# Three more slabs of a mixer split in parts, and the first transfers and products of the kernel rearranged

## The reference, cut to what matters

```python
x = first_block(...)        # rms_norm, w_in, three attentions, gates, w_out, MLP
# second block
xn = rmsnorm(h, mix_norm_w)
proj = xn @ w_in
xa, qkv, z, beta_logit, a_logit, gate_a, gate_b = split(proj)
y_a = pool_mixer(xa, pool_w, pool_scale) @ w_pool_up      # trailing means over 2, 4, 8, 16 tokens
y_b = deltanet_branch(qkv, z, beta_logit, a_logit, ...) @ w_dn_up   # causal conv, silu, l2norm, delta rule
merged = sigmoid(gate_a) * y_a + sigmoid(gate_b) * y_b
h = h + merged @ w_mix_out
h = h + peer_ffn(rmsnorm(h, ffn_norm_w), ...)             # 128 expert rows a token
return rmsnorm(h, final_norm_w)
```

## Time and profile before

| what | value |
|---|---|
| median of three runs | 1455.67 us |
| the profiled execution | 1455.38 us |
| its span on the core | 1453.6 us |
| TensorE busy | 1302.1 us, 90% of the span |
| VectorE busy | 899.7 us, 62% |
| GpSimd busy | 645.7 us, 44% |
| ScalarE busy | 460.9 us, 32% |
| chain that ended last | 58% TensorE, 28% DMA |

### The profile page before, as it was taken

How to read it: one execution, slowest core, us unless ns; L and a number is a source line. 1 busy time by engine, 2 the same in 40 slices (tenths; PEclk the granted TensorE clock), 3 DMA queues, 4 the chain that set the end, 5 groups by cost and what they waited for, 6 DMA issues and landing times.

```text
span 1453.6 us, 17543 instructions
## 1 busy us (share of the span) xinstructions
PE 1302.1 (90%) x6502; PEld 947.6 (65%) x6502; DVE 899.7 (62%) x1720; ACT 460.9 (32%) x843; POOL 645.7 (44%) x394
## 2 busy tenths in 40 slices
PE   5999998999989999999999997788878898776877
PEld 5997987998879999999975553344334443232332
DVE  3244244999945966432627776676776777667654
ACT  3664524444344534112101322222222222222222
POOL 5553235889936613321203534443444445444430
PEclk9999999999999999999999999999999999999998
DMA  7724343445543433122406999999999999999994
GB/s 264 288 86 168 117 158 132 174 174 199 207 174 117 174 146 117 65 110 88 141 34 266 422 423 420 422 421 422 422 421 421 422 421 421 421 422 421 422 421 170
DMA packets 54203, 389.90 MB, mean 268 GB/s; under 512 B 5208, under 2 KB 13544, under 8 KB 14440
## 3 DMA queue, kind: packets, MB, share of 16 engines
q0 software_dynamic: 36864, 268.45, 44.4%
q1 hardware_dynamic: 14720, 116.40, 21.4%
q10 hardware_dynamic: 2536, 3.95, 0.8%
HBM read 387.70 MB, written 1.07 MB: 267 GB/s over the span
## 4 chain that ended last, share of the span: by engine, by line
PE 58%; DMA 28%; DVE 5%; issue 3%; POOL 2%; ACT 1%; ACTq 0%; DVEq 0%; POOLq 0%
PE psum L506 57%; DMA work<-experts_dram,work 21%; DMA weight_ring<-experts_dram,work 6%; DVE work L1747 2%; POOL work L2329 1%; PE psum L675 1%; ACT work L2161 0%; POOL weight_ring L2329 0%; DMA bias_rows_dram<-work 0%; ACT work L1972 0%; DVE work L1544 0%; PE psum L903 0%; DVE work L1736 0%; DVE work L1734 0%; POOL norm_stats L2234 0%
## 5 line engine op out<-in xcount | busy, mean ns | idle before, releaser
L506 PE MATMUL psum<-work 128*128 128x128 f32 (+6 forms) x1880 | 446.7, 394 | 65.0 <-ACT work L2161 64.7
L506 PEld LDWEIGHTS psum<-work 128*128 128x128 f32 (+2 forms) x1880 | 265.7, 193 | 236.9 <-issue 150.8
L2244 POOL TENSOR_TENSOR weight_lo<-weight_ring,weight_hi 128x2048 fp32r<-128x2048 f32 x62 | 291.9, 4708 | 175.8 <-ACT weight_hi L1827 159.9
L2329 POOL DMA_INDIRECT work<-experts_dram,work x153 | 171.3, 1119 | 216.7 <-PE psum L506 180.4
L1747 DVE CUSTOM_DVE_ANT_0 work<-work 128x1024 f32<-128x1024 f32 x153 | 187.5, 1226 | 109.7 <-DMA work<-experts_dram,work 96.7
L506 PE MATMUL psum<-weight_ring,work 128*128 128x512 f32 (+1 forms) x448 | 200.8, 593 | 42.1 <-ACT work L2161 42.1
L506 PEld LDWEIGHTS psum<-weight_ring,work 128*128 128x128 f32 (+1 forms) x448 | 81.6, 186 | 147.9 <-issue 85.6
L506 PE MATMUL psum<-normed_T,weight_ring 128*128 128x256 f32 (+1 forms) x768 | 156.5, 362 | 1.7 <-ACT normed_T L1827 1.7
L1827 ACT ACTIVATE weight_hi<-weight_ring 128x2048 fp32r<-128x2048 f32 x66 | 125.8, 1915 | 89.6 <-DMA weight_ring<-weights_dram 79.3
L506 PEld LDWEIGHTS psum<-normed_T,weight_ring 128*128 128x128 f32 x768 | 135.6, 190 | 22.8 <-issue 5.3
L506 PE MATMUL psum<-mlp_in_hi,weight_hi 128*128 128x256 f32 x504 | 144.9, 290 | 5.6 <-POOL weight_lo L2244 5.6
(11 more groups left out here) (263 smaller groups left out, 1736.9 us busy)
## 6 DMA issues: line engine op xcount, KB each, us to landing
weight_ring<-weights_dram SPq DMA_DIRECT2D x50, 2048.0 KB, 7.9
work<-weights_dram SPq DMA_DIRECT2D x3, 1024.0 KB, 6.4
work<-experts_dram,work POOLq DMA_INDIRECT x153, 20.3
weight_ring<-weights_dram SPq DMA_DIRECT2D x2, 1024.0 KB, 13.4
gain_rows<-gains_dram SPq DMA_DIRECT2D x2, 1024.0 KB, 10.2
work<-bias_rows_dram ACTq DMA_DIRECT2D x2, 1024.0 KB, 10.5
weight_ring<-experts_dram,work POOLq DMA_INDIRECT x80
constants<-constants_dram ACTq DMA_DIRECT2D x1, 1094.0 KB, 9.5
```

The lines of the kernel that those rows point to most:

```text
L506: return nc.tensor.matmul(o, l, r, start=start, stop=stop)
L2244: G_.tensor_tensor(low, loaded, high.bitcast(F32), ALU.subtract).then_inc(S("weight_lo_ready"), 1)
L2329: G_.indirect_dma_start(out=slots[s], out_offset=None, in_=experts, in_offset=bass.IndirectOffsetOnAxis(ap=expert[:, n % UNIT_BUFS, i:i + ...
```

## The change

In the second mixer:

- xa, gate2_b0 and gate2_b1 are multiplied split too. Six halves (66 to 71) are added, each with a high part by ScalarE and a low part by GpSimd. Their homes are 22528, 26624, 24576, 16480, 0 and 2048 of `work`.
- u2_hi moves to offset 12384 of `work`, u2_lo to the area of the gain rows. The second transfer of the gains moves from slab 40 to slab 44 and waits for gate2_b1.
- The gate logits (`beta_a`) and the first two square sums are computed in parts of 64 tokens.

At the start:

- x is loaded in two transfers, one for each tile. ScalarE squares each tile; there is a root for each; VectorE makes a scaled diagonal of 128 x 128, and TensorE multiplies the residual by it. `normed` and the functions `mean_squares` and `scaled` go.
- VectorE makes both parts of half 0. ScalarE makes u_hi, VectorE u_lo.
- The first projection goes through `first_features`, in the order high·high, low·high, high·low, each group with its own waits.
- The large part of the constants is loaded on SP behind slab 1, not on ScalarE's queue at the start.
- k_att is computed ahead of the bias rows, on TensorE and on ScalarE.

The words that came with the change say that the input's two transfers are joined; the diff has one transfer before and two after, and the diff is what is taken here.

```diff
-    + tuple((31 + s, f"qkv{s}", "features") for s in range(6))
+    + tuple((31 + s, f"qkv{s}", "features") for s in range(6)) \
+    + ((37, "xa", "features"), (38, "gate2_b0", "features"), (39, "gate2_b1", "features"))
+XA_HALF = QKV_HALF + 12
-DVE_HALVES = (5, MLP_HALF + 1, QKV_HALF, QKV_HALF + 1)
+DVE_HALVES = (0, 5, MLP_HALF + 1, QKV_HALF, QKV_HALF + 1)
-    + [(22528, 26624, 24576)[h % 3] for h in range(SPLIT_HALVES - QKV_HALF)]
+    + [(22528, 26624, 24576)[h % 3] for h in range(XA_HALF - QKV_HALF)] + [22528, 26624, 24576, 16480, 0, 2048]
-    u2_hi = split_part("mixer_in_hi", "work", 18528, [P, KC, SEQ])
-    u2_lo = split_part("mixer_in_lo", "work", 16480, [P, KC, SEQ])
+    u2_hi = split_part("mixer_in_hi", "work", 12384, [P, KC, SEQ])
+    u2_lo = split_part("mixer_in_lo", "gain_rows", 0, [P, KC, SEQ])
...
+            def first_features(name, after):
+                for i in range(2):
+                    h = next_half()
+                    _, lo, hi = half_views(h)
+                    ps = open_bank(name, i)
+                    if h == 0:
+                        pe.wait_ge(S("vector_weight_hi_ready"), 1)
+                    else:
+                        pe.wait_ge(S("weight_hi_ready"), h)
+                    for a in range(2):
+                        f, o = slice(a * P, (a + 1) * P), ps[:, a * SEQ:(a + 1) * SEQ]
+                        for k in range(KC):
+                            if i == a == 0 and k % 2 == 0:
+                                pe.wait_ge(S("mix_hi_ready"), k // 2 + 1)
+                            mm(o, hi[:, k, f], u_hi[:, k, :], k == 0, False)
+                        if a == 0:
+                            low_ready(h)
+                        for k in range(KC):
+                            mm(o, lo[:, k, f], u_hi[:, k, :], False, False)
+                        for k in range(KC):
+                            if i == a == 0 and k % 2 == 0:
+                                drained(pe, after, k // 2)
+                            ins = mm(o, hi[:, k, f], u_lo[:, k, :], False, k == KC - 1)
+                    close_bank(ins, name, i)
+                slab_read(name, 1)
...
-            transposes("mix_T", normed, norm=0)
-            split_features("q_nsa", after="mix_T")
+            transposes("mix_T", h_tok, norm=0, scale=mix_scale)
+            first_features("q_nsa", "mix_T")
+            split_features("k_att", groups=3)
...
-                        if s < 2:
-                            ins = mm(ps[:, cols], square_buf[:, s % 2, a, t * P:(t + 1) * P], C("ones")[:, 0:2])
-                        else:
-                            for c in range(2):
...
+                        for c in range(2):
+                            tokens, r = slice(t * P + c * CHUNK, t * P + (c + 1) * CHUNK), (c if s < 2 else 1 - c) * CHUNK
+                            ins = mm(ps[r:r + CHUNK, cols], square_buf[:, s % 2, a, tokens], C("ones")[:, 0:2])
...
-            feature_major("xa", uT, KC)
+            split_features("xa", src=(u2_hi, u2_lo))
...
-            feature_major("gate2_b0", uT, KC)
+            split_features("gate2_b0", src=(u2_hi, u2_lo))
...
-            feature_major("gate2_b1", uT, KC)
+            split_features("gate2_b1", src=(u2_hi, u2_lo))
...
@@ scalar @@
-                    if s < 4 or (s, i) == (4, 0):
-                        weight_high(QKV_HALF + 3 + 2 * s + i)
+                    weight_high(QKV_HALF + 3 + 2 * s + i)
...
             for i in range(2):
                 ps = full(act, "xa", i).rearrange("p (a n) -> p a n", a=2)
                 free(copy(xa[:, 2 * i:2 * i + 2, 16:272], ps), "xa", i)
+                if i == 0:
+                    weight_high(XA_HALF + 3)
             silu(5)
+            weight_high(XA_HALF + 4)
...
             A.activation(k_dec, k_dec, ACT.Exp).then_inc(S("e_factors_ready"), 1)
             landed(act, "e_factors_ready")
+            weight_high(XA_HALF + 5)
...
@@ gpsimd @@
-            for h in range(DVE_HALVES[3] + 1, SPLIT_HALVES):
+            for h in range(DVE_HALVES[4] + 1, XA_HALF):
                 weight_low(h)
             for kind in range(2):
+                for h in ((XA_HALF, ), (XA_HALF + 1, XA_HALF + 2))[kind]:
+                    weight_low(h)
                 drained(pool, f"ssq{2 * kind + 1}")
...
+            for h in range(XA_HALF + 3, SPLIT_HALVES):
+                weight_low(h)
...
@@ sync @@
-            sp.dma_start(h_tok[:, :, :], x.rearrange("(t p) d -> p t d", p=P)).then_inc(S("x_loaded"), 16)
+            for t in range(TT):
+                sp.dma_start(h_tok[:, t, :], x[t * P:(t + 1) * P, :]).then_inc(S(f"x{t}_loaded"), 16)
...
+                if n == 1:
+                    sp.dma_start(cst[:, FIRST_CONST:], consts[:, FIRST_CONST:]).then_inc(S("more_constants_loaded"), 16)
...
-                if n == 40:
-                    drained(sp, "mlp_out", 3)
+                if n == 44:
+                    full(sp, "gate2_b1", 1)
```

More of the change, by code:

```diff
@@ L1181, in settle @@
                 dve.wait_ge(S("vector_chain"), chained[0])
[L1183 to L1200, removed]
             def scale_diagonal(n, t, dst):
@@ L1246, in _, with vector_weight_low @@
             landed(dve, "cmp_act_zero")
-            dve.wait_ge(S("x_loaded"), 16)
-            mean_squares(0, h_tok, range(TT), work[:, 4096:4096 + D])
-            rstd_done(dve, 0)
-            for t in range(TT):
-                scaled(0, t, h_tok, normed)
-            dve.wait_ge(S("parameters_loaded"), 16)
+            def vector_weight_low(h):
+                if h:
+                    dve.wait_ge(S("weight_hi_ready"), h)
+                loaded, low, high = half_views(h)
+                V.tensor_tensor(low, loaded, high.bitcast(F32), ALU.subtract).then_inc(S("vector_weight_lo_ready"), 1)
+                landed(dve, "vector_weight_lo_ready")
+            for t in range(TT):
+                scale_diagonal(0, t, mix_scale)
+            dve.wait_ge(S("first_half_loaded"), 16)
+            loaded, low, high = half_views(0)
+            V.tensor_copy(high, loaded).then_inc(S("vector_weight_hi_ready"), 1)
+            landed(dve, "vector_weight_hi_ready")
+            vector_weight_low(DVE_HALVES[0])
             g_mix = PR("g_mix")
@@ L1255, in _ @@
                 ps = full(dve, "mix_T", i)
[L1256 to L1259, removed]
+                dve.wait_ge(S("mix_hi_ready"), i + 1)
                 for a in range(2):
@@ L1851, in drain_T_high @@
                     last.then_inc(S("u_hi_ready"), 1)
-            weight_high(0)
+            for t in range(TT):
+                act.wait_ge(S(f"x{t}_loaded"), 16)
+                A.activation(work[:, 4096:4096 + D], h_tok[:, t, :], ACT.Square, scale=D ** -0.5, accum_out=stat[:, 0, 0, t:t + 1]).then_inc(S("input_squares"), 1)
+                landed(act, "input_squares")
+            act.wait_ge(S("parameters_loaded"), 16)
+            g_mix = PR("g_mix")
+            for i in range(4):
+                ps = full(act, "mix_T", i)
+                for a in range(2):
+                    c = 2 * i + a
+                    last = copy(u_hi[:, c, :], ps[:, a * SEQ:(a + 1) * SEQ], g_mix[:, c:c + 1])
+                last.then_inc(S("mix_hi_ready"), 1)
             weight_high(1)
-            full(act, "mix_T", 3)
             weight_high(2)
@@ L1861, in _ @@
                 weight_high(3 + i)
+            ps = full(act, "k_att", 0)
+            free(copy(k_att[:, 0:2, :].rearrange("p a n -> p (a n)"), ps), "k_att", 0)
+            weight_high(5)
+            ps = full(act, "k_att", 1)
+            free(copy(k_att[:, 2, :], ps[:, 0:SEQ]), "k_att", 1)
+            weight_high(6)
             for table in range(2):
@@ L1872, in _ @@
                     .then_inc(S(f"toeplitz{table}_loaded"), 16)
-            ps = full(act, "k_att", 0)
-            free(copy(k_att[:, 0:2, :].rearrange("p a n -> p (a n)"), ps), "k_att", 0)
-            weight_high(5)
-            ps = full(act, "k_att", 1)
-            free(copy(k_att[:, 2, :], ps[:, 0:SEQ]), "k_att", 1)
-            weight_high(6)
             for t in range(TT):
@@ L2245, in weight_low @@
                 landed(pool, "weight_lo_ready")
-            rstd(0)
+            for t in range(TT):
+                rstd(0, t)
             for h in range(OUT_HALF + 2):
```

40 lines of the change are left out of this document (18 added, 22 removed).

## The result

| | before | changed |
|---|---|---|
| median | 1455.05 us (20 runs, 1453.57 to 1458.05) | 1459.87 us (20 runs, 1455.45 to 1467.08) |
| ratio, from all runs | | 1.0042, 95% interval 1.0031 to 1.0053 (the medians alone give 1.0033) |
| the profiled execution | 1455.38 us | 1455.45 us, span 1453.7 us |
| VectorE, GpSimd busy | 899.7, 645.7 us | 915.5, 677.3 us |

The change makes the kernel 0.3 to 0.4% slower; forecast were 1458.4 us and "slower" with 0.53. The profiled execution is the lowest of the twenty, and the times of the changed kernel lie in two heaps: 13 between 1455.45 and 1461.14 us, 7 between 1465.48 and 1467.08 us. The kernel before has no second heap. So the trace of this one run can't explain the upper heap.

The account below looks back on a forecast made before the run. TensorE was taken to bound the kernel up to the first expert fetch, with fetches behind shifting as a whole. 1455.38 us less 5.5 us (start) plus 8.5 us (second mixer) gave 1458.4 us; 8 in 10 range 1448 to 1464.5 us.

Parts of the forecast that it names:

- the start: Kernel start through the first attention: 5.5 us earlier, bounds 3 to 7.7 us, the gain carried on to all behind.
- the second mixer: Second mixer, gate logits to chunk products: 8.5 us longer, bounds 2.4 to 12 us, from GpSimd passes and lower clock.
- TensorE's first split product: Start of the first projection: at about 14.5 us in place of 20.13 us, wrong if past 17 us.
- The softmax: First attention: starts at about 51 us in place of 54.45 us, once the first table has landed.
- the transposes of the probabilities: First attention: come at about 62.2 us in place of 67.7 us, after half 8's pass ends at about 58 us.
- The walk: Second mixer step by step, taps and passes excluding each other: pooling done at 553.3 us, gate2_b1 at 570.1 us, +6.7 us.
- TensorE's two waits: Second mixer: TensorE waits 2.6 us for the squares of s=3 and 9 us for gate2_b0's second half.
- The clock: Second mixer: idle times put TensorE at its lower clock for half of one 3.5 us stretch, +1.8 us.
- The forms of 64 tokens: Second mixer on TensorE: first two square sums 1.3 us less, gate logits 1.4 us less.
- A: Second mixer: the passes hide and TensorE keeps its 9.8 us gain, 1440.1 us in all; chance 0.08.
- B: Passes and taps pack to the bound, clock stays up, start at its better end: 1451.9 us, 1449 to 1455; chance 0.25.
- C: Start gives nothing back because the first table lands late, past 54 us: 1463.4 us in all; chance 0.15.

Follow-up runs that it names:

- 1: The changed kernel with the second mixer's edits undone, so only the start differs from the kernel before: median 1452.46 us, ratio 0.9979.
- 7: Only the start of the change, with ScalarE making the high part of half 8 behind the first exponentials: median 1449.44 us, ratio 0.9963 to the kernel before.
- 5: The changed kernel with the high part of half 8 made behind the first exponentials, so GpSimd's pass comes later: median 1454.39 us.
- 2: The kernel before with only the second mixer's edits of the change: median 1462.79 us, ratio 1.0043.
- 9: The changed kernel run again unaltered, for another profile: median 1459.15 us over 8 runs; its profiled run took 1451.90 us.
- 10: The changed kernel run once more unaltered, for another profile: median 1462.87 us over 6 runs; its profiled run took 1464.70 us.
- 3: The changed kernel without GpSimd's passes for halves 66 to 71, the high part read in place of the low: median 1444.09 us.
- 6: The changed kernel with half 8's high part behind the first exponentials and the low parts of halves 66 to 71 made by VectorE: median 1445.50 us.
- 11: As 7, plus the second mixer's gate logits and first two square sums in parts of 64 tokens: median 1447.84 us.
- kernel 4: The changed kernel with the low parts of halves 66 to 71 made by VectorE in place of GpSimd: median 1450.25 us.

## Why the prediction was right, and where it was not

The forecast of 1458.4 us stood 1.5 us from the median, and that it came so near is luck: its sum has two errors of opposite sign, the second mixer too slow and the start, with its catch, too fast. By the medians:

| step | predicted | found |
|---|---|---|
| the start | -5.5 us | -3.1 us as changed (1 against before); -5.6 us with nothing in its way (7 against before) |
| the second mixer | +8.5 us | +5.0 us (5 against 7); +7.2 us alone (2 against before) |
| L1310 caught, TensorE idle, the clock | not a term of its own | +5.5 us (changed against 5) |

The profiles of 5 and 7 give 6.7 us for the second mixer: from the boundary to VectorE's first step on kk (L1560) it is 566.91 - 423.48 = 143.4 us in 5 and 560.37 - 423.65 = 136.7 us in 7. So 5 to 7 us is as near as it gets, and my 8.5 us was 1.5 to 3.5 us too much. The other profiles with the split fit: from the boundary to the k_tok transposes, by the chain, it is 136.6 us (9), 137.4 us (changed), 138.5 us (10) and 138.7 us (2), against 131.9 us before.

**The start.** TensorE's first split product: 14.5 us said, 12.91 us found. VectorE had both parts of the first half at 12.29 + 2.29 = 14.6 us, as said, but the first products need the high part alone, and the products with the diagonal were done by then: they ran at the full clock, both tiles in 5.51 us, where I had taken 3.5 us a tile from the lower level. The softmax: 51 us said, 49.75 us found. TensorE reached the first scores at 46.44 us, where I said 45.5 us. Then the step that failed, though its place was right: "in the changed kernel the pass of half 8 ends at about 58 us, so the transposes of the probabilities ... come at about 62.2 us". The pass ended at 58.83 us and the transposes came at 63.19 us. What I didn't ask is what TensorE has to do until then. It ran out of work at 61.1 us, and an idle time there is costly, as the boundary had shown; I priced the clock in the second mixer and not here. Nor did I ask whether the step must meet the pass at all: it does so or not by 0.1 us. And -5.5 us was said of a course with L1310 caught; the course with that catch and nothing worse gives -4.5 us at the transposes, the free one -7.1 us (60.61 against 67.7 us). The -5.6 us of kernel 7 agrees with my number, not with its reason; the start as it was changed is worth 3.1 us in the median.

**The second mixer.** The walk holds where it can be compared. My times less the 5.0 us of the boundary, and the found ones: taps of the fourth slab done at 508.7 (508.3), of the fifth at 525.1 (524.2), of the sixth at 532.2 (531.4); halves 69 and 70 at 540.4 and 545.3 (539.5 and 544.4); pooling 548.3 (546.8); end of gate2_b1 565.1 (564.1 us). TensorE's two waits, 2.6 and 9 us, were 2.37 and 8.11 us. That GpSimd's passes and VectorE's work between SBUF operands exclude each other was the mechanism, as 3 and 6 show. The Trainium skill, in "SBUF — State Buffer", Who interferes with whom, adds that copy and tensor_scalar can take the ports shared with GpSimd too, with one input in SBUF, where their operands allow a mode with two ports. L1310 (0.17 or 3.8 to 4.4 us) and L1524 (0.29 or 4.47 us) agree, and I had applied its rule to taps and pooling alone.

Three terms were sized wrong. The clock, +1.8 us, cost at most 0.4 us that the end sees. It fell behind the 2.37 us wait, but the 8.11 us wait came after that; and it fell within the 8.11 us wait and was low in the second half of gate2_b0, which pooling nearly covered (pooled values at 546.81 us, TensorE's products with them from 547.17 us):

```profile
513.00:516.00 3.00, 3.00 (x16) 3.00 (x15) 3.00 (x3) 2.23 (x2) 2.91 (x1) 0.50 0.66 270
```

```profile
533.00:540.00 7.00, 0.44 (x2) 0.44 (x3) 6.88 (x6) 3.15 (x5) 6.84 (x3) 0.53 0.00 0
540.00:544.00 4.00, 4.00 (x22) 4.00 (x22) 3.98 (x1) 0.00 (x0) 4.00 (x1) 0.54 0.00 0
```

The forms of 64 tokens were worth 1.6 us and not 2.7 us: the square sums gave 1.84 - 1.10 = 0.74 us a slab, near my 0.67 us, the gate logits 0.1 us in 11 and 0.2 to 0.4 us elsewhere (3.64 us against 3.58 us and 3.28 to 3.41 us), not 1.4 us. I had taken 64 records at the 32 ns of the square sums; here they took 51 to 56 ns each. And pooling was done 1.5 us before my time.

**The rivals.** A (the passes hide, 1440.1 us) is refuted by 3: leaving them out gives 1444.09 us, 16 us below the changed kernel, so they do not hide. B (1451.9 us) named a time that some runs have, for another reason than its own: pooling ended at 546.81 us, 1.5 us ahead of the walk but 2.9 us behind the bound of 548.9 - 5.0 = 543.9 us that B needs. C did not happen, since the table came at 49.75 us. What the catch of L1310 costs, 5.5 us of the median, was in no rival. My range held the median, but not the seven runs of the second heap.

## What to carry to other kernels

Before work is added to GpSimd or moved in time, look for the small VectorE steps between an engine's product and the next (row maxima, negations, copies): one of 0.17 us costs what is left of a pass if it is due in one (3.8 to 4.4 us here). Price each of them by what TensorE still has to do at that time, and if it has nothing, add what the clock does behind the gap. If the times of a kernel fall into heaps, take a profile from each before explaining any; and where passes and VectorE's own work exclude each other anyway, VectorE makes the pass in half the time (2.29 us in place of 4.6 us), as in the best version here:

```profile
502.17 2.29 DVE L1269 TENSOR_TENSOR weight_lo<-weight_ring,weight_hi 128x2048 fp32r<-128x2048 f32 x1
...
506.45 5.09 DVE L1477 SCALAR_TENSOR_TENSOR work<-work,parameters 128x256 f32<-128x256 f32 x12
...
511.78 4.62 DVE L1269 TENSOR_TENSOR weight_lo<-weight_ring,weight_hi 128x2048 fp32r<-128x2048 f32 x2
...
518.38 5.09 DVE L1477 SCALAR_TENSOR_TENSOR work<-work,parameters 128x256 f32<-128x256 f32 x12
```

## What the runs showed of the hardware

TensorE's clock stayed at half for 16 us and more behind waits of 2.83 and 2.85 us, although products followed each other without a break; behind a wait of 4.29 us it was back at full within 12 us, behind one of 2.73 us in kernel 3 the same 16 us had a mean of 0.89, behind one of 2.08 us it never fell, behind one of 2.37 us (the changed kernel's second mixer) it was low for a few microseconds, and so it was behind the 3.82 us of the boundary and behind the gate logits, where TensorE had not been idle at all. What decides between these stays open: the length of the wait alone does not. That the long stretch makes the second heap rests on two profiled runs with it (1457.02 us in kernel 4, 1464.70 us in 10), on no profiled run with the changed start that lay above 1460 us without it, and on the heap's absence in 5, 6 and 7; no profile was had of the one run of 1460.14 us in 5. The mean granted clock of each run points the same way, but weakly: it is 0.960 on average over the changed kernel's 12 runs above 1464 us and 0.963 over its other 22, where the profiled runs of 9, of the first profile and of 10 have 0.966, 0.962 and 0.956. So for most runs of the upper heap the long stretch is likely and not shown.
